# An expert turn in another order, with equal token tiles and five of its weight splits on GpSimd

## The reference, cut to what matters

```python
for e in range(N_EXPERTS):          # 8 experts, D_FF_EXPERT = 1408
    y = y + gates[..., e:e + 1] * _swiglu(h, w_g[e], w_u[e], w_d[e])
def _swiglu(h, wg, wu, wd):
    return (jax.nn.silu(h @ wg) * (h @ wu)) @ wd
```

## Time and profile before

| what | value |
| --- | --- |
| median of three runs | 2531.6 us (2523.83 to 2531.7) |
| the profiled execution's own time | 2531.62 us |
| its span, first to last instruction | 2529.7 us |
| TensorE busy | 2216.4 us, 88% |
| VectorE busy | 1219.0 us, 48% |
| ScalarE busy | 899.8 us, 36% |
| GpSimd busy | 154.6 us, 6% |

### The profile page before, as it was taken

The page is one execution under the profiler, slowest core; times in us unless marked ns, Lnnn a source line. Parts: engine busy times, 40 slices in busy tenths (PEclk is TensorE's granted clock), DMA queues, the critical chain, the costliest instruction groups (busy, mean ns, idle before and its releaser), DMA issues.

```text
span 2529.7 us, 37510 instructions
## 1 busy us (share of the span) xinstructions
PE 2216.4 (88%) x15366; PEld 2037.6 (81%) x15366; DVE 1219.0 (48%) x1736; ACT 899.8 (36%) x1298; POOL 154.6 (6%) x155
## 2 busy tenths in 40 slices
PE   5898688868999999889859778599999999999997
PEld 5888477858999998878749668488888888898885
DVE  4543424443332332643433453446766766657563
ACT  5422132423221222441122423245444454444442
POOL 2022000030000001002200030000000000000000
PEclk9998778779999999898868888779999999999998
DMA  3200011112332232110001111135645555455551
GB/s 123 77 26 18 18 34 52 42 44 66 93 101 84 92 101 80 51 60 18 17 18 44 59 43 60 42 117 168 200 146 176 161 171 183 143 167 168 167 176 42
DMA packets 60609, 230.59 MB, mean 91 GB/s; under 512 B 7208, under 2 KB 7608, under 8 KB 60496
## 3 DMA queue, kind: packets, MB, share of 16 engines
q1 hardware_dynamic: 57168, 219.77, 27.2%
q0 software_dynamic: 3328, 9.17, 1.2%
HBM read 223.00 MB, written 5.91 MB: 90 GB/s over the span
## 4 chain that ended last, share of the span: by engine, by line
PE 76%; DVE 14%; ACT 6%; issue 4%; DMA 0%; DVEq 0%; SPq 0%; ACTq 0%
PE ps L551 74%; DVE sb_s L1518 2%; DVE sb_s L1526 2%; ACT sb_s L1077 2%; DVE sb_w_lo L2091 2%; ACT L1077 1%; DVE sb_y L1518 1%; ACT sb_w_hi L1069 1%; DVE sb_h_lo L1518 1%; DVE sb_w_lo L1509 1%; PE ps L629 1%; DVE sb_afg L2125 0%; ACT sb_y L1077 0%; DVE sb_sel_t L1522 0%; ACT sb_gb L1077 0%
## 5 line engine op out<-in xcount | busy, mean ns | idle before, releaser
L551 PE MATMUL ps<-sb_h_hi,sb_w_hi 128*128 128x260 f32 x1952 | 578.6, 296 | 45.3 <-DVE sb_h_lo L1518 28.4
L551 PE MATMUL ps<-sb_h_hi,sb_w_lo 128*128 128x260 f32 x1952 | 564.2, 289 | 0.0
L551 PE MATMUL ps<-sb_h_lo,sb_w_hi 128*128 128x260 f32 x1952 | 564.2, 289 | 0.0
L551 PEld LDWEIGHTS ps<-sb_h_hi,sb_w_hi 128*128 128x128 f32 x1952 | 382.8, 196 | 55.3 <-issue 40.0
L1471 ACT ACTIVATE sb_w_hi<-sb_w_raw 128x1024 fp32r<-128x1024 f32 (+1 forms) x241 | 275.8, 1144 | 395.6 <-PE ps L551 394.7
L551 PE MATMUL ps<-sb_hg,sb_w_hi 128*128 128x320 f32 x1408 | 389.9, 360 | 19.8 <-DVE sb_w_lo L2091 17.7
L551 PEld LDWEIGHTS ps<-sb_h_lo,sb_w_hi 128*128 128x128 f32 x1952 | 382.7, 196 | 2.5 <-issue 1.8
L551 PEld LDWEIGHTS ps<-sb_h_hi,sb_w_lo 128*128 128x128 f32 x1952 | 381.8, 196 | 0.0
L1509 DVE TENSOR_TENSOR sb_w_lo<-sb_w_raw,sb_w_hi 128x1024 fp32r<-128x1024 f32 (+1 forms) x140 | 177.6, 1270 | 397.6 <-ACT sb_w_hi L1069 397.5
L1069 ACT ACTIVATE sb_w_hi<-sb_w_raw 128x1024 fp32r<-128x1024 f32 (+1 forms) x140 | 153.1, 1094 | 593.5 <-PE ps L551 593.4
L551 PE MATMUL ps<-sb_hg,sb_w_lo 128*128 128x160 f32 x1408 | 336.1, 239 | 0.0
(11 more groups left out here) (258 smaller groups left out, 2892.3 us busy)
## 6 DMA issues: line engine op xcount, KB each, us to landing
sb_w_raw<-in_wgu SPq DMA_DIRECT2D x223, 512.0 KB, 3.6
sb_w_raw<-in_wd SPq DMA_DIRECT2D x80, 704.0 KB, 4.7
sb_w_raw<-in_wz SPq DMA_DIRECT2D x62, 512.0 KB, 3.5
sb_w_raw<-in_wo SPq DMA_DIRECT2D x16, 512.0 KB, 3.6
sb_x<-in_xT SPq DMA_DIRECT2D x8, 260.0 KB, 4.9
out_y<-sb_y SPq DMA_DIRECT2D x8, 260.0 KB, 2.2
sb_y<-in_gS POOLq DMA_DIRECT2D x2, 512.0 KB, 3.6
out_gS_s<-sb_y POOLq DMA_DIRECT2D x2, 512.0 KB, 2.9
```

The costliest lines, as they stand in the source:

```text
L551: return pe.matmul(out, lhsT, rhs, start=start, stop=stop, skip_group_check=True)
```

## The change

Tokens are cut into five equal tiles of TT = 104 instead of 128 and a rest of 8, in the router, the gather and the gate columns. `Yrest` grows from 64 to 96 rows; its last 32 rows are set to zero once, in the router, and their slot number is 0.5, which no token has.

The scatter of the turn before moves from iterations f = 2 to 5 into the down loop, one tile behind each gather, all in one pair of PSUM banks. The 16 transposes of a turn move into the next turn, behind its f = 1; ScalarE's high parts follow its f = 2, VectorE's low parts f = 3; keys of the turn before follow f = 4, its key matmuls f = 6 and its slot matrices f = 7. Gate columns stay with the turn itself. Turn 1 is written out as well, and behind the last turn the steps from the transposes to the slot matrices stand ahead of the scatter.

GpSimd writes the low part of units 2, 6, 10, 14 and 18 of each turn; VectorE skips them, and TensorE and SP wait on GpSimd's semaphore for those units.

```diff
+TT = TOK // 5
+POOL_E = (2, 6, 10, 14, 18)
-        Yrest = sb("yg_rest", [2 * REST, D], F32R, experts)
+        Yrest = sb("yg_rest", [3 * REST, D], F32R, experts)
+        def lo_ready(eng, it, i):
+            it, i = it + i // EU, i % EU
+            mine = sum(1 for u in POOL_E if u <= i)
+            if i in POOL_E:
+                eng.wait_ge(sem["wlo_g"], it * len(POOL_E) + mine)
+            else:
+                eng.wait_ge(sem["w_lo"], it * (EU - len(POOL_E)) + (E0 + i + 1 - mine))
...
+            with pool.Fori(0, final + 1) as it:
+                for i in POOL_E:
+                    hi, lo = split_e(i)
+                    pool.wait_ge(sem["w_hi"], it * EU + (E0 + i + 1))
+                    inc(pool.tensor_tensor(lo[:, 0:KT * P], raw_e(i)[1][:, 0:KT * P], hi[:, 0:KT * P].bitcast(F32),
+                                           ALU.subtract), "wlo_g")
...
-                        last = mm(PS[:, GATHER_BANK[k % 4], part * CAP:(part + 1) * CAP], h[0:n, i, k * P:(k + 1) * P],
-                                  SelG[0:n, i, :], i == 0, i == 4)
+                        last = mm(PS[:, GATHER_BANK[k % 4], part * CAP:(part + 1) * CAP], h[0:TT, i, k * P:(k + 1) * P],
+                                  SelG[0:TT, i, :], i == 0, i == 4)
...
-                        last = mm(out, Yrest[:, f], SelT[0:2 * REST, 1, t], False, True)
+                    last = mm(out, Yrest[:, f], SelT[0:3 * REST, 1, t], False, True)
...
-                    if before is not None and 2 <= f < 6:
-                        scatter(before, range(2 * f - 4, 2 * f - 2))
+                    if before is not None and f == 1:
+                        slots_first(before)
                     if f == 6:
...
+                            key_rows(before)
+                        gate_cols(it)
                 for m in range(KT):
                     gather(it + 1, m)
...
+                        scatter(before, m)
+                    lo_ready(pe, it, 2 * GF + m)
...
+                    if before is not None and f == 2:
+                        slots_high(before)
...
             def split_turn(it, i):
                 i += 2
+                if i in POOL_E:
+                    return
...
-                    if before is not None and 2 <= f < 6:
-                        add(before, range(2 * f - 4, 2 * f - 2))
+                    if before is not None and f == 3:
+                        slots_low(before)
                     if f == 4:
-                        keys(e, it)
+                        if before is not None:
+                            keys(before if isinstance(before, int) else before % EXPERTS, before)
                     if f == 7:
...
+                            slots_of_tokens(before)
+                        gate_cols(it)
                     if f == 8:
                         select(e1, it + 1)
                 for m in range(KT):
+                    if before is not None:
+                        add(before, m)
```

More of the change, by code:

```diff
@@ L886, in router @@
                 for i in range(5):
[L887 to L889 removed]
+                    out = M[3][0:8, i * TT:(i + 1) * TT] if i < 4 else M[2][0:8, 0:TT]
+                    last = pe.transpose(out, KEY[0:TT, i, :], ident[0:TT, 0:TT])
                 inc(last, "rt_p")
@@ new lines, in key_rows, with gate_cols @@
+            def key_rows(it):
+                pe.wait_ge(sem["ktm_v"], it + 1)
+                pe.wait_ge(sem["ylo_v"], it * 2 + 2)
+                for h in range(2):
+                    last = mm(PS[:, 4 + h, 0:HALF], ones[32:40, :], KTM[:, h * HALF:(h + 1) * HALF])
+                inc(last, "key_p")
+            def gate_cols(it):
+                for st, n in SLOTS:
+                    for t in range(5):
+                        last = mm(PS[0:n, 6, 2 * st:2 * st + 2], SelG[0:TT, t, st * P:st * P + n],
+                                  GE[0:TT, t, :], t == 0, t == 4)
+                inc(last, "key_p")
@@ L1052, in _ @@
             turn(0)
-            with pe.Fori(0, final) as before:
+            turn(1, 0)
+            with pe.Fori(1, final) as before:
                 turn(before + 1, before)
+            slots_first(final)
+            key_rows(final)
+            pe.wait_ge(sem["selt_v"], final * 2 + 2)
             for m in range(KT):
-                scatter(final, [m])
+                if m >= 2:
+                    pe.wait_ge(sem["xadd_v"], final * KT + (m - 1))
+                scatter(final, m, 4 + 2 * (m % 2))
                 if m:
@@ L1498, in _ @@
             split_turn(0, -1)
-            with act.Fori(0, final[0] + 1) as it:
-                turn(it)
+            turn(0)
+            turn(1, 0)
+            with act.Fori(1, final[0]) as before:
+                turn(before + 1, before)
+            slots_high(final[0])
             rn(LAYERS, 4)
@@ L2175, in _ @@
             turn(0)
-            with dve.Fori(0, final) as before:
+            turn(1, 0)
+            with dve.Fori(1, final) as before:
                 turn(before + 1, before)
-            add(final, range(KT))
+            slots_low(final)
+            keys(final % EXPERTS, final)
+            slots_of_tokens(final)
+            for m in range(KT):
+                add(final, m, 4 + 2 * (m % 2))
             rn(LAYERS, 4)
```

167 lines of the change are left out of this document (82 added, 85 removed).

## The result

The changed kernel takes 2472.36 us (median of four runs, 2466.38 to 2475.06) against 2531.62 us on the same chip: ratio 0.977, 95% interval 0.9743 to 0.9797. That is faster by 59 us where 25 were forecast; the time lies in the whole range and outside the forecast's own. The profiled execution's span is 2472.4 us, 57.3 less than before.

A forecast was written before the change was run, and what follows sets the result against it. TensorE's own instructions were taken to set the pace, busy 99.6 of a 102.6 us turn. Turns -27, first gather -6, tail -3 and clock +11 gave -25 us: 2506 us, own range 2490 to 2525, whole range 2460 to 2546.

The forecast's parts named there:

- Rows: Gather and scatter matmuls on TensorE: equal tiles and a 96-row rest save 10.4 us a turn.
- the surcharge: TensorE's extra time when matmul row counts change: 0.24 us per gather five, 0.385 us per scatter triple.
- tail: Stretch after the last turn: steps now in series cost 4 us, 16 triples save 6.2 and more; -3 us.
- The rival that 96 rows pay as 64 do: Scatter in the down loop: triples keep the 0.385 us extra, 50 us in all, giving 2556 us; chance 0.11.
- The hold: VectorE's two-SBUF-input operations, short products included, stop until GpSimd's subtraction of some 2.3 us ends.
- The first rival: Gate-and-up stretch: VectorE's short products are not held beside GpSimd, giving 2464 us; chance 0.14.
- The walk: Step-by-step working of VectorE and GpSimd per unit: TensorE waits 11.1 us a turn against 4.0, 7.1 more.
- eight turns give -27: All eight turns: the -3.3 us sum of one turn applied to each, -27 us.
- Clock: One more half-clock dip, 1.6 us, in each of seven turns, from longer TensorE waits: +11 us.
- The third rival: Clock stays at half for long in the waits, three dips a turn: 2517 to 2528 us; chance 0.10.
- ahead of turn 0: The gather before the first turn: saves 3.9 us at full clock, twice that at half; taken as -6.
- the sum of a turn: One turn: -10.4 us of rows plus 7.1 us more of TensorE waits, -3.3 us.

The follow-up runs named there:

- e2: The kernel before with only 104-token tiles and a 96-row rest, in its old order and without GpSimd's share: 2427.74 us.
- e3: The changed kernel with the third matmul of each scatter triple back at 64 rows: 2529.04 us.
- e7: The changed kernel without GpSimd's share, plus five two-input GpSimd subtractions a turn on scratch tiles nobody waits for within a turn: 2498.19 us.
- e9: The changed kernel with the gate columns one iteration later (f = 7 instead of 6): 2455.26 us.
- e11: The changed kernel with GpSimd held back by some 0.7 us ahead of its subtraction for unit 14: 2462.8 us.
- e4: The new order alone: old tiles of 128 and 8 tokens, a 64-row rest, all subtractions on VectorE: 2570.96 us.
- e1: The changed kernel with all 22 low weight parts back on VectorE, none on GpSimd: 2435.8 us.

## Why the prediction was right in kind and wrong in size

*Rows: right, a tenth too small.* Forecast 10.4 us a turn, measured 11.5 with nothing else changed (e2). The gather saves 5.0 instead of 3.9, as the unit behind its second five started late as well: the surcharge is paid on the way out too (e3), and the working took the fives alone. The tail's rows were taken as 6.2 us and more, and are 11.2. The rival that 96 rows pay as 64 do falls (triples 0.36 us apart); e3 shows what it would have cost. The Trainium skill (TensorEngine Tiling (Array Packing), "Tiling Modes") lists modes of 128, 64 and 32 rows and a drain when the mode changes. It does not say in which mode 96 and 104 rows run; the trace agrees with the working, which took them as 128.

*The hold: right, also for short products.* Those beside GpSimd take 2.52 us. The first rival named 2464 us, close to the result, by a mechanism that is not there: its closeness is luck. The Trainium skill (SBUF — State Buffer, "Who interferes with whom") has whoever issues first hold the other; both orders stand in the rows above, 0.12 us and 0.17 us apart.

*The walk: right in its places, and this is where the sum first fails.* 11.1 us of waits were forecast for every turn, 10.4 stand in a looped one, at the places named (2.80 before unit 11 for 3.1; 2.05 and 0.80 for 2.9 before units 12 and 13; 2.7 before units 19 and 20 for 3.8 from unit 17 on). A looped turn without its stretch of half clock is 97.4 us: -5.2, not -3.3. But "eight turns give -27" charged the whole sum to all eight. Turn 0 has no low outputs, keys or slots: its TensorE stands 1.7 us (84.96 - 83.24) where a looped one stands 8.3, and turn 1 stands 6.0. Turn 0 has no scatter either, so the sum counted the 6.2 us of the triples nine times, in eight turns and the tail, where they run eight times. It fell by 10.8 us instead of 3.3, in part because its transposes (2.4 us with their wait) and key rows now run in turn 1 and it lost a stretch of half clock.

*Clock: the second step that fails.* The working took "one dip more in each of seven turns: 7 x 1.6 = +11". There are six stretches in the eight turns, as before (the working read four there). The trace of before had them behind the key matmuls, not behind waits, and the working moved the cause to the waits. Waits have a part in it in other kernels: in e7 every turn from turn 1 on has a stretch during or behind each of the two times in which TensorE stands idle for 4.3 and 3.1 us, and e9 and e11 have some behind the 2.80 us wait. In the changed kernel that wait, 2.6 us of idle TensorE, has none behind it. The third rival, long times at half clock, does not hold either: the turns of the changed kernel have a granted clock of 0.97 to 1.00.

By stretches, forecast and measured: ahead of turn 0 -6 and -6.6; turn 0 -3.3 and -10.8; turns 1 to 7 -23 + 11 = -12 and -35.0; tail -3 and -4.8. Mis-sized, then, are the sum of a turn, with its multiplication by eight, and the clock term; the tail is two larger terms that cancel (rows -11.2, new order +6.4).

What the forecast never asked was what each part does alone. Its own terms had it: -10.4 of rows beside +7.1 of order and GpSimd.

## What to carry to other kernels

When a change bundles parts of opposite sign, price and run each alone: here one of three parts beats the whole by 45 us. Before giving an elementwise subtraction to GpSimd, look at what VectorE runs beside it; if both read two SBUF tiles they take turns, and the lost time lands on whichever instruction starts second, critical or not. Multiply a turn's sum only by the turns that have all its terms, and count changes of a matmul's row count on the way out as on the way in.

## What was not expected of the hardware

- A GpSimd operation with one input (2.85 us for 128 x 1024) holds VectorE's two-input operations only at its start: such an operation that starts 0.54 us after it loses 0.44 us, one at 0.67 loses 0.30, at 0.83 0.06, at 2.0 nothing; one that starts 1.03 us after a GpSimd operation which had itself been held 0.9 us loses 0.84. With two inputs the loss reaches to GpSimd's end (2.2 us for a start at 0.85 of 3.19). The Trainium skill (SBUF — State Buffer, "Who interferes with whom") lets a VectorE instruction with two SBUF inputs contend with any GpSimd instruction that reads SBUF, and gives the shared ports to whoever issues first for the whole instruction. That is what the runs show for two inputs; for one input these rows decide otherwise.
- A difference of 0.17 us in who starts first is worth 2 us of a turn (96.9 and 97.1 us in e11 against 99.0, with one stretch of half clock in each). A stretch of half clock can turn that order: e9 has two stretches more than the changed kernel and takes 17 us less.
- The clock falls without a wait ahead of it, too: with 64-row and 8-row matmuls ahead of every down unit (e4) the granted clock fell two or three times in the down loop of each turn with a scatter (0.94 over a turn), with 96 and 104 rows at the same places (e1) never. It takes both: with 64 and 104 rows (e3), and with 8-row gathers and no scatter there (the kernel before), it never fell in the down loop.
